# A two-layer transformer trunk on one core: the first column chunk multiplied in unsplit float32, and the first branch cut into chunks of 512, 384 and 262 columns

## What is computed

```python
def _mixer(x, w_in, b_f, w_pa, w_pb, w_pc, w_o):
    hcat = jnp.einsum('bsd,de->bse', x, w_in)            # 6,662 columns
    qa, ka, va, fa, qb, kb, vb, qc, kc, vc, g = jnp.split(hcat, offsets, axis=-1)
    ya = _fox_attention(_heads(qa, 6), _heads(ka, 6), _heads(va, 6), fa + b_f)
    yb = _dilated_attention(...)
    yc = _moba_attention(...)
    gates = jax.nn.sigmoid(g).reshape(bsz, s, 3, D_MODEL)
    merged = sum of gates[b] * (y[b] @ w_p[b])
    return merged @ w_o

x = _layer_norm(x, ln_in_g, ln_in_b)
for l in range(2):
    x = _layer_norm(1.414 * x + _mixer(x, ...), ln1_g[l], ln1_b[l])
    x = _layer_norm(1.414 * x + _swiglu(x, ...), ln2_g[l], ln2_b[l])
```

## Time and profile before

| | |
|---|---|
| median of 3 runs | 865.18 us (864.96 to 866.91) |
| time of the profiled execution | 865.8 us |
| its span, first to last instruction | 864.0 us |
| TensorE busy | 847.9 us, 98% |
| VectorE busy | 494.7 us, 57% |
| ScalarE busy | 415.9 us, 48% |
| GpSimd busy | 62.6 us, 7% |
| moved by DMA | 149.36 MB, 173 GB/s on average |
| TensorE's granted clock | 0.996 of full on average |

### The profile page before, as it was taken

The page is one execution under the profiler, slowest core; times in us unless marked ns, Lnnn a source line. Parts: engine busy times, 40 slices in busy tenths (PEclk is TensorE's granted clock), DMA queues, the critical chain, the costliest instruction groups (busy, mean ns, idle before and its releaser), DMA issues.

```text
span 864.0 us, 10890 instructions
## 1 busy us (share of the span) xinstructions
PE 847.9 (98%) x4280; PEld 704.0 (81%) x4280; DVE 494.7 (57%) x681; ACT 415.9 (48%) x569; POOL 62.6 (7%) x103
## 2 busy tenths in 40 slices
PE   8989999999999999999999999999999999999996
PEld 7878888888877888888888889888888788888885
DVE  6755464556676545445565656463766664555434
ACT  5665465553355344444346655554454553344421
POOL 0022331000000000000000324200000000000000
PEclk9999999999999999999999999999999999999999
DMA  7774433456637665664436443435754576556601
GB/s 268 241 253 152 135 121 115 144 183 231 194 100 266 222 192 186 200 194 153 157 110 231 141 155 111 145 100 167 243 198 146 195 250 201 187 190 190 200 1 49
DMA packets 93618, 149.36 MB, mean 173 GB/s; under 512 B 3584, under 2 KB 52992, under 8 KB 93568
## 3 DMA queue, kind: packets, MB, share of 16 engines
q1 hardware_dynamic: 93568, 148.67, 52.8%
HBM read 147.60 MB, written 1.05 MB: 172 GB/s over the span
## 4 chain that ended last, share of the span: by engine, by line
PE 89%; DVE 5%; DMA 2%; ACT 2%; issue 2%; POOL 0%; POOLq 0%; DVEq 0%; ACTq 0%
PE bank L1165 79%; PE bank L1180 3%; PE bank L1224 3%; PE bank L1256 2%; DVE w_lo L942 2%; DMA raw<-in_w_in 1%; PE bank L1244 1%; PE bank L1190 1%; ACT w_hi L823 1%; DVE x L1125 1%; DVE act_lo L948 1%; DVE x L1054 1%; DMA x<-in_x 0%; DVE stats L1084 0%; ACT act_hi L840 0%
## 5 line engine op out<-in xcount | busy, mean ns | idle before, releaser
L942 DVE TENSOR_TENSOR w_lo<-raw,w_hi 128x2048 fp32r<-128x2048 f32 (+3 forms) x143 | 309.1, 2166 | 91.4 <-ACT w_hi L823 90.8
L1165 PE MATMUL bank<-w_hi,act_hi 128*128 128x512 f32 (+2 forms) x864 | 341.9, 396 | 0.0
L1165 PE MATMUL bank<-w_hi,act_lo 128*128 128x512 f32 (+2 forms) x864 | 332.5, 385 | 0.0
L1165 PE MATMUL bank<-w_lo,act_hi 128*128 128x512 f32 (+2 forms) x864 | 331.4, 384 | 0.0
L823 ACT CAST w_hi<-raw 128x2048 fp32r<-128x2048 f32 (+3 forms) x143 | 257.3, 1802 | 102.6 <-PE bank L1165 80.1
L1165 PEld LDWEIGHTS bank<-w_hi,act_lo 128*128 128x128 f32 x864 | 162.3, 188 | 32.8
L1165 PEld LDWEIGHTS bank<-w_hi,act_hi 128*128 128x128 f32 x864 | 162.6, 188 | 29.4
L1165 PEld LDWEIGHTS bank<-w_lo,act_hi 128*128 128x128 f32 x864 | 162.8, 188 | 28.6
L1165 PE MATMUL bank<-w_hi,y_hi 128*128 128x512 f32 x240 | 95.3, 397 | 0.0
L1165 PE MATMUL bank<-w_hi,y_lo 128*128 128x512 f32 x240 | 93.7, 390 | 0.0
L1165 PE MATMUL bank<-w_lo,y_hi 128*128 128x512 f32 x240 | 93.5, 390 | 0.0
(11 more groups left out here) (106 smaller groups left out, 584.4 us busy)
## 6 DMA issues: line engine op xcount, KB each, us to landing
raw<-in_w_in SPq DMA_DIRECT2D x47, 1024.0 KB, 5.2
raw<-in_w_gate SPq DMA_DIRECT2D x44, 512.0 KB, 3.9
raw<-in_w_up SPq DMA_DIRECT2D x44, 512.0 KB, 4.9
raw<-in_w_down SPq DMA_DIRECT2D x22, 1024.0 KB, 4.9
raw<-in_w_o SPq DMA_DIRECT2D x8, 1024.0 KB, 5.5
raw<-in_w_in SPq DMA_DIRECT2D x4, 768.0 KB, 4.5
raw<-in_w_pa SPq DMA_DIRECT2D x4, 768.0 KB, 4.3
raw<-in_w_pc SPq DMA_DIRECT2D x4, 768.0 KB, 4.5
```

The costliest lines, as they stand in the source:

```text
L942: dve.tensor_tensor(weights(w_lo, i, HI_SLOTS), weights(raw, i, RAW_SLOTS), weights(w_hi, i, HI_SLOTS).bitcast(F32), ALU.subtract).then_in ...
L1165: ins = pe.matmul(bank[use[0]][:, 0:width], a, w[:, k, c0:c0 + width], start=start and k == 0 and p == 0, stop=stop and k == nk - 1 and p ...
```

## The change

Chunk 0 of layer 0 is no longer split. Its 2 MB of raw weights go in four quarters into memory that the attention uses later (`shared`, `act_fns`), and the rows, transposed and copied to `merged`, are multiplied by them in plain float32: one matmul for each of 8 row blocks of the weights and each row tile, 16 in all (L1213 of the new kernel), where 48 stood. The first norm is made tile by tile (`first_norm`): gain and bias come as four rows (`in_norms`), are spread over 128 partitions by eight matmuls with an inner dimension of 4 (`spread_rows`), and VectorE applies them to the rows before they are transposed. GpSimd makes the inverse square root by a power, VectorE does one round of the iteration. The step `affine` and its loads go. The split of the rows (`split_rows`), which the later chunks need, comes after the first products. Zeros are multiplied 12 and 14 times in place of 48 and 16. In both layers chunk 1 has 384 columns in place of 512, and chunk 2 has 262 in place of 134.

```diff
-    (512, 512, [("qk", 0, 4, 256), ("v", 0, 0, 256)]),
-    (1024, 134, [("v", 0, 256, 128), ("f", 0, 0, FOX_HEADS)]),
+    (512, 384, [("qk", 0, 4, 256), ("v", 0, 0, 128)]),
+    (896, 262, [("v", 0, 128, 256), ("f", 0, 0, FOX_HEADS)]),
...
-WARM = (48, 16)
+WARM = (12, 14)
+QUARTERS = 4
...
+    def turn_rows(t):
+        for j in range(2):
+            turned["first", t, j] = aux_bank()
+            plan.append(("turn_rows", t, j, turned["first", t, j]))
+
+    def split_rows(t):
+        plan.append(("split_rows", t))
+        turned[t, 0] = turned[t, 1] = ("rows", t + 1)
...
+    spread_rows = [[bank(2 + 2 * a + j) for j in range(2)] for a in range(2)]
     plan.append(("warm", WARM[0]))
-    turn_x(0, 0)
-    split_lo()
+    plan.append(("spread_rows", spread_rows))
     plan.append(("warm", WARM[1]))
...
+    plan.append(("first_norm", 0, spread_rows))
+    turn_rows(0)
+    plan.append(("first_norm", 1, spread_rows))
...
         if layer == 0:
-            for c in range(2):
-                for t in range(TT):
-                    if (c, t) == (0, 1):
-                        for _ in range(HI_SLOTS - 2):
-                            split_hi()
-                    use0 = bank(2 * c + t)
-                    for half in range(2):
-                        if (c, t, half) == (0, 0, 1):
-                            turn_x(1, 0, 1)
-                        if (c, t) == (1, 0):
-                            plan.append(("affine", half, turned[half, 1]))
-                        qkv(c, t, (half,), use0, t == TT - 1, False)
+            for t in range(TT):
+                use0 = bank(t)
+                for quarter in range(QUARTERS):
+                    if t == 0 and quarter == QUARTERS - 1:
+                        turn_rows(1)
+                        split_hi()
+                        split_lo()
+                        split_rows(0)
+                    plan.append(("first_mm", t, quarter, use0, turned["first", t, quarter // 2]))
+                qkv_done(0, t, use0)
+                if t == 0:
+                    split_rows(1)
+                    split_hi()
+                    split_lo()
+                    for _ in range(HI_SLOTS - 2):
+                        split_hi()
+                flush()
+            for t in range(TT):
+                use0 = bank(2 + t)
+                for half in range(2):
+                    qkv(1, t, (half,), use0, t == TT - 1, False)
...
+        first_raw = [(shared, act_fns)[q // 2][:, (q % 2) * 1024:(q % 2 + 1) * 1024].rearrange("p (k n) -> p k n", k=2)
+                     for q in range(QUARTERS)]
...
+        rows_hi, rows_lo = w_hi[HI_SLOTS - 1][0:4, 0:NW], w_lo[HI_SLOTS - 1][0:4, 0:NW]
+        row_pick = w_hi[HI_SLOTS - 1][0:4, NW:NW + 4]
...
                 sp.dma_start(gain_bias[:, 0, :], g.partition_broadcast(P)).then_inc(gb_loaded, 16)
                 sp.dma_start(gain_bias[:, 1, :], b.partition_broadcast(P)).then_inc(gb_loaded, 16)
 
             last_probs = None
-            for t in range(TT):
-                sp.dma_start(x[t][:, :], d["x"][t * P:(t + 1) * P, :]).then_inc(x_loaded[t], 16)
-            norms, put_off = 0, None
+
+            def load_first(q):
+                src = d["w_in"][0, 2 * q * P:2 * (q + 1) * P, 0:NW].rearrange("(k p) n -> p k n", p=P)
+                sp.dma_start(first_raw[q], src).then_inc(first_loaded[q], 16)
+
+            sp.dma_start(norm_rows, d["norms"]).then_inc(norms_loaded, 16)
+            sp.dma_start(x[0][:, :], d["x"][0:P, :]).then_inc(x_loaded[0], 16)
+            load_first(0)
+            sp.dma_start(tables[:, 0:P], d["tables"][:, 0:P]).then_inc(ident_loaded, 16)
+            load_first(1)
+            sp.dma_start(x[1][:, :], d["x"][P:2 * P, :]).then_inc(x_loaded[1], 16)
+            load_first(2)
+            load_first(3)
+            norms, put_off = TT, None
...
+                    if i == RAW_SLOTS:
 
                         sp.dma_start(tables[:, P:], d["tables"][:, P:TABLE_COLS]).then_inc(tables_loaded, 16)
-                        sp.dma_start(merged[0][:, 0:SEQ + FOX_HEADS], d["tables"][:, TABLE_COLS:]
+                        sp.wait_ge(rows_lo_done, 1)
+                        sp.dma_start(squares_out[:, 0:SEQ + FOX_HEADS], d["tables"][:, TABLE_COLS:]
...
-            pool.wait_ge(tables_loaded, 48)
             squares = 0
+            tables_known = False
             for step in PLAN:
+                if step[0] in ("spread", "sum") and not tables_known:
+                    pool.wait_ge(tables_loaded, 48)
+                    tables_known = True
...
+                elif step[0] == "first_norm":
+                    t = step[1]
+                    pool.wait_ge(first_var, t + 1)
+                    pool.tensor_tensor(rstd[:, t:t + 1], var_eps[:, t:t + 1], exponent[:, :],
+                                       ALU.pow).then_inc(first_root, 1)
...
-                            ins = act.activation(source_rows[:, k * P:(k + 1) * P], bank[b][:, k * P:(k + 1) * P],
-                                                 ACT.Identity, bias=norm_cols[:, 1, dk + k:dk + k + 1],
-                                                 scale=norm_cols[:, 0, dk + k:dk + k + 1])
...
+                elif kind == "spread_rows":
+                    act.wait_ge(norms_loaded, 16)
+                    act.copy(w_hi[HI_SLOTS - 1][0:4, 0:NW + 4], norm_rows).then_inc(rows_hi_done, 1)
+                elif kind == "turn_rows":
+                    _, t, j, (b, n) = step
+                    act.wait_ge(filled[b], n)
+                    act.copy(merged[t][:, j * NW:(j + 1) * NW], bank[b][:, :]).then_inc(drained[b], 1)
+                elif kind == "split_rows":
+                    t = step[1]
+                    for j in range(2):
+                        b, n = first_turns[t, j]
+                        act.wait_ge(drained[b], n)
+                    act.copy(hi["act"][:, :, t * P:(t + 1) * P], group_view(merged[t], KT, P)).then_inc(first_hi, 1)
...
+                elif kind == "spread_rows":
+                    dve.wait_ge(rows_hi_done, 1)
+                    dve.tensor_tensor(rows_lo, norm_rows[:, 0:NW], rows_hi.bitcast(F32),
+                                      ALU.subtract).then_inc(rows_lo_done, 1)
+                elif kind == "first_norm":
+                    _, t, (gain, bias) = step
+                    one = slice(t, t + 1)
+                    dve.wait_ge(x_loaded[t], 16)
+                    for nh in range(2):
+                        mark(dve.bn_stats(stats[:, t, nh, :], x[t][:, nh * NW:(nh + 1) * NW]))
                     settle()
-                    for t, _ in uses:
-                        mark(dve.bn_aggr(mean_var[:, t, :], stats[:, t, :, :]))
+                    link(dve.bn_aggr(mean_var[:, t, :], stats[:, t, :, :]))
+                    dve.tensor_scalar(var_eps[:, one], mean_var[:, t, 1:2], LN_EPS, None,
+                                      ALU.add).then_inc(first_var, 1)
+                    mark(dve.tensor_scalar(half_var[:, one], mean_var[:, t, 1:2], LN_EPS, -0.5, ALU.add, ALU.mult))
+                    for nh, (b, n) in enumerate(gain):
+                        xh = x[t][:, nh * NW:(nh + 1) * NW]
+                        dve.wait_ge(filled[b], n)
+                        ins = dve.scalar_tensor_tensor(out=xh, in0=xh, scalar=mean_var[:, t, 0:1], in1=bank[b][:, :],
+                                                       op0=ALU.subtract, op1=ALU.mult)
+                        if t:
+                            ins.then_inc(drained[b], 1)
+                        else:
+                            mark(ins)
                     settle()
...
+                    if t:
+                        for b, n in gain:
+                            dve.wait_ge(drained[b], n)
+                    dve.wait_ge(first_root, t + 1)
+                    link(dve.scalar_tensor_tensor(out=newton[:, one], in0=rstd[:, one], scalar=half_var[:, one],
+                                                  in1=rstd[:, one], op0=ALU.mult, op1=ALU.mult))
+                    link(dve.scalar_tensor_tensor(out=rstd[:, one], in0=newton[:, one], scalar=1.5, in1=rstd[:, one],
+                                                  op0=ALU.add, op1=ALU.mult))
+                    for nh, (b, n) in enumerate(bias):
                         xh = x[t][:, nh * NW:(nh + 1) * NW]
-                        dve.tensor_scalar(xh, xh, mean_var[:, t, 0:1], rstd[:, t:t + 1], ALU.subtract,
-                                          ALU.mult).then_inc(x_ready, 1)
+                        dve.wait_ge(filled[b], n)
+                        dve.scalar_tensor_tensor(out=xh, in0=xh, scalar=rstd[:, one], in1=bank[b][:, :], op0=ALU.mult,
+                                                 op1=ALU.add).then_inc(x_ready, 1)
+                    dve.wait_ge(x_ready, 2 * (t + 1))
+                    if t:
+                        for spare, (b, n) in zip((row_sum[:, 0, 0:1], row_sum[:, 0, 1:2]), bias):
```

(32 more changed lines are left out.)

144 lines of the change are left out of this document (44 added, 100 removed).

## The result

The changed kernel takes 870.01 us, the median of 4 runs (869.54 to 870.33), against 866.01 for the kernel before (4 runs, 864.96 to 866.91): ratio 1.0050, 95% interval 1.0037 to 1.0064. It is 4.0 us slower; against the medians of 865.5 to 865.6 that the kernel before took beside the experiments it is 4.4 to 4.5. The forecast was 866.8 and the range 863.4 to 870.2. Its profiled execution took 870.33 us, 4.5 more than that of before.

What follows compares the result with a forecast made beforehand. TensorE was taken as the bound, busy 847.9 of 864.0 us. Terms: +1.5 at layer 0's first scores, -1.2 in layer 1, +0.5 and +0.8 for the clock, +1.6 in all: 866.8 us, range 863.4 to 870.2.

Steps and rivals of the forecast that it cites:

- part 6: Low clock after TensorE's idling: 0.5 us lost at the start, 0.8 behind the second stall.
- part 5: Waits at forget sum and scores absorb delay: layer 0's first scores 1.5 us late, layer 1 gains 1.2.
- Part 1: Start of the kernel: first product near 10.7 instead of 14.87, 4.2 us earlier, the spread lying under the statistics.
- Part 2: First chunk: float32 products of 0.91 us each, then TensorE stalls 2.4 us for ScalarE's copy of tile 0's result.
- Part 3: Second stall, after tile 1's products: TensorE waits 4.9 us for ScalarE's copy behind piece 4's cast and load.
- Part 4: Chunks 1 and 2 with the new widths: 2.2 us less in each layer, 15.0 us with transposes.
- The low clock through the first chunk: Rival: first products run at the low clock and cost double, up to 5.5 us more; 868 to 871, chance 0.2.
- A dear float32 product: Rival: first-chunk float32 products cost near the upper end, 1.6 us each; 870.4 us, chance 0.1.
- Faster, stall not formed: Rival: second stall does not form, chunk 3 starts at 44.5, both layers keep the widths' saving; 862.0 us, chance 0.12.
- Nothing moves but the beginning: Rival: layer 0's waits take up all they can, layer 1 keeps all; 864.5 us, inside the range, no own chance.

Runs made afterwards that it cites:

- e9: The changed kernel measured once more, unedited: 868.64 us, ratio 1.0041 to the kernel before.
- e3: The changed kernel with ScalarE's casts of weight pieces 2, 3 and 4 moved behind the copy of row tile 1's chunk 0 result: 866.21 us, ratio 0.9994.
- e10: The changed kernel with 48 matmuls on zeros added on TensorE inside the second stall: 867.34 us, ratio 1.0022.
- e4: The changed kernel with 20 zero matmuls in place of 12 before the spread: 868.63 us, ratio 1.0028.
- e2: The changed kernel with the old widths (512, 512, 134) in both layers: 872.99 us, ratio 1.0074.
- e13: The changed kernel with the forget sum's cast ahead of two weight casts on ScalarE, in both layers: 868.14 us, ratio 1.0026.
- e1: The kernel before with only the new widths (512, 384, 262) in both layers: 864.78 us, ratio 0.9986.
- e7: The changed kernel with low parts of pieces 2 and 3 before chunk 0's qk_lo, and only piece 4's cast behind tile 1's copy: 863.05 us, ratio 0.9955.
- e8: As e7, plus 20 zeros in place of 12 and the transposes of chunk 0's result put off: 860.68 us, ratio 0.9939.
- e12: e8 with the forget sum's cast ahead of two weight casts on ScalarE in both layers: 858.97 us, ratio 0.9923.

## Why the prediction was right and wrong

The direction and the two stalls were right. The size was not: +1.6 forecast, +4.0 measured by the medians (+4.5 by the profiled executions, +3.1 in the second measurement, e9). The step that failed is part 6, what the low clock costs: 0.5 taken for the start, 2.1 measured; 0.8 taken behind the second stall, 2.7 measured. Beside it the gain of layer 1 (part 5) was 0.4 and not 1.2.

**Part 1, the start, right in its sum but not in its cover.** The forecast put the first product at 10.7. Where the clock rises early it is at 10.3; in the profile compared here it is at 12.78. The failed step is the sentence that the spread "lies under the statistics": it gave the spreads no length and left out the 14 zeros that stand behind them in TensorE's queue. At the high clock this does no harm, at the low one the queue runs until 11.05. Part 6 held 0.5 us for a start at the low clock; it costs 2.3 in the profile compared here.

**Part 2.** Float32 product: 0.91 taken, 0.86 measured (16 records from 23.73, eight in 3.43 us, two to a product). The bounds of 0.46 and 1.6 were far from it, the argument from four part products was right; the Trainium skill's rule (FP8 and Floating Point Precision, TensorE Precision Notes) of four passes agrees with this trace, where an ordinary product takes 0.23. First stall: 2.4 forecast, 1.81 measured.

**Part 3, right.** Forecast 4.9, measured 4.96 and 5.56. Its working holds link by link: low part of piece 1, load at once, 5.2 us, cast, `qk_hi`, copy. e3 undid the link that the forecast named as the cause and the stall fell to 0.68. The stall is not cushioned: in the profile after it starts 3.1 us later than in e9 and ends 2.5 later. Its length goes with the load: 5.3 us from issue to cast in the first profile, 5.9 in e9.

**Part 4, right.** The 262-column products are 0.12 apart, as the two rows from the timeline after, six products apart, show (0.72 us in between), and chunks 1 and 2 take 15.1 us at the high clock (e10), forecast 15.0.

```profile
47.51 0.28 PE L1232 MATMUL bank<-w_lo,act_hi 128*128 128x262 f32 x1
...
48.23 0.28 PE L1232 MATMUL bank<-w_lo,act_hi 128*128 128x262 f32 x1
```

**Part 6, the clock, the term that was mis-sized most.** Forecast 0.8 after the gap, with 1.7 as a bound, because before the low clock had lasted 3.4 us. After the longer stall it lasted 6.8 us (34.6 to 41.4), and 2.6 us of work were lost. Taking the one duration in the trace as an upper bound was the mistake. The longer idle time is not the whole reason, though. Behind 5.27 us of idling in e4 and 5.56 in e9 the low clock lasted 6.8 us as well; but it lasted 3.4 behind 4.10 in e2, and also behind 5.02 in e13, although e13's plan up to there is that of the changed kernel:

```profile
32.75 1.12 PE L1260 MATMUL bank<-tables,stage 128*128 128x128 f32 x4 [5.02 <-ACT stage L881]
```

```profile
32.00:33.00 1.00, 0.25 (x1) 0.26 (x2) 0.69 (x1) 0.69 (x2) 0.00 (x0) 0.66 0.00 0
...
35.00:36.00 1.00, 1.00 (x5) 1.00 (x4) 1.00 (x2) 0.00 (x0) 0.00 (x0) 0.63 0.00 0
```

By these rows the clock fell 0.4 us before TensorE went on in e13; in the changed kernel, e4 and e9 it had fallen 1.1 to 1.5 us before. From the transposes to chunk 3 e13 takes 16.5 us, so the forecast's bound of 1.7 would have held there. What decides between the two lengths is not shown.

**Part 5.** Chunk 3 came 7.9 us late, not 3.4. The waits that were to absorb took 2.7, against 1.9 forecast of a smaller delay: with everything late, both go whole, as the bound of 1.0 assumed. First scores: +5.2, forecast +2.8 with the clock's terms. Layer 1: forecast 1.2 gained of 2.2, measured 0.4 (0.3 in e9, 1.25 in e1). The reason given was right, a sum that hangs on ScalarE and a load, and e13 confirms it; but its chain of 10.8 us starts behind the cast of a load that has just landed, and how far this landing moves with TensorE (29.4 us behind the row transposes before, 28.9 after, 28.1 in e1) was not to be read from one trace. Why it differs from kernel to kernel by a microsecond stays open.

In numbers, by the profiled executions: +1.6 forecast, +1.6 for the start (12.78 against 10.7, less the 0.5 held), -0.3 for the first products and stalls, +1.9 for the clock behind the stall, -0.8 that the old waits took more, +0.8 for layer 1, and -0.3 between and behind: +4.5.

**The rivals.** *The low clock through the first chunk*, 868 to 871.3 with a chance of 0.2: this is what the first profile shows in its weaker form (from 14 us on the float32 records are 0.43 apart), with the low clock behind the stall added to it. The measured time lies in its range, but not by its mechanism alone: the first eight records took 4.17 us in place of 3.43, so the products at the low clock cost 0.7, where the rival had up to 5.5; the other 2.1 us are the queue and the transposes in front of them. The Trainium skill's rule that the low level is the default and activity lifts it (TensorE: Matmul & The Clock Gate, Part 1) agrees with e9's start; in the first profile TensorE worked without a hole from 1.33 on and the level rose only near 14, which the rule by itself does not give. That the rise comes at another time in another execution of the same program no row of before had shown. *A dear float32 product* fell with 0.86. *Faster, stall not formed* fell for this kernel, but is what e7 and e8 became: once the late load stands behind the copy, chunk 3 starts at 43.42 and 41.37, even sooner than the rival's 44.5. *Nothing moves but the beginning* fell.

## What to carry to other kernels

When a beginning is rewritten, follow each engine's queue to the instruction that the bottleneck waits for, and ask which item ahead of it waits for a load: here one copy behind one cast cost 5 us of idling and up to 2.6 of low clock. Moving casts behind the copy brought the kernel back to the time of before (e3), the low parts in their place made it 2.5 us faster (e7), and all orders together 5 to 7 us (e8, e12). A saving upstream of a wait is worth only what the wait's own chain moves; find that chain's rigid stretch and shorten it first (10.8 us here; the edit that made it 9.4 took the wait away, but its 0.5 to 1.9 us are not clear of the noise). Cost a new stall at its idle time plus the low clock behind it, and don't take the only low stretch of the old trace as the bound. When one execution can start 2.3 us later than another of the same kernel, compare profiled executions by landmarks and not by their spans.

## What the runs showed of the hardware

- The granted clock's rise at the start is not fixed: in two executions of the same kernel the same matmuls, started at the same 4.19 us, ran 0.43 and 0.23 us apart. The first products came at 12.78 and 10.34, and the span differed by 2.3 us. The profile's clock column reads 1.00 in that stretch in both, so the spacing of starts is the better witness there.
- After an idle time of 4.96 us (after), 5.27 (e4) and 5.56 (e9) the low level lasted 6.8 us (in the trace after, 5.7 of them with TensorE working); after 2.02, 2.36 (e1), 4.10 (e2) and 5.02 (e13) it lasted about 3.4. Behind the 1.81 us of the first stall the float32 records of the changed kernel kept their 0.43 us, so the clock did not fall.
- A float32 product of 512 columns is two records of 0.43 us, 0.86 in all, 3.7 times the 0.23 of an ordinary one; in the 64-column case it was 0.20.
